# A two-block transformer in float32: the last phase worked by token tile, weights split in place, the expert loop's end rearranged

## What is computed

```python
x = x + hier_moe(rms_norm(x, ffn_norm), ...)          # experts
x = rms_norm(x, final_norm)
for i in range(2):
    h = x @ w_in[i]                                   # 7 or 10 chunks of 256 columns
    mix = gmlp_mixer(u, v, ...) if i == 0 else moba_attention(q, k, v)
    mem_out = memory_cross_attention(q_mem, mem, w_mem_kv[i])
    sub = concatenate([mix, mem_out]) @ w_mix_out[i]
    x = layer_norm(ALPHA * x + sub, ln_mix_g[i], ln_mix_b[i])
    g, u = split(x @ w_ffn_in[i])
    x = layer_norm(ALPHA * x + (silu(g) * u) @ w_ffn_out[i], ln_ffn_g[i], ln_ffn_b[i])
```

## Time and profile before

| | us |
|---|---|
| median of 3 runs | 1829.1 |
| runs, lowest to highest | 1827.12 to 1831.46 |
| the profiled execution's own time | 1827.96 |
| its span (first to last instruction) | 1826.5 |
| PE busy (matmuls) in the span | 1409.8, 77% |
| DVE, ACT, POOL busy | 605.9, 412.3, 58.6 |

### The profile page before, as it was taken

How to read it: one execution, slowest core, us unless ns; L and a number is a source line. 1 busy time by engine, 2 the same in 40 slices (tenths; PEclk the granted TensorE clock), 3 DMA queues, 4 the chain that set the end, 5 groups by cost and what they waited for, 6 DMA issues and landing times. The chain is left out here.

```text
span 1826.5 us, 21480 instructions
## 1 busy us (share of the span) xinstructions
PE 1409.8 (77%) x9510; PEld 988.7 (54%) x9510; DVE 605.9 (33%) x777; ACT 412.3 (23%) x551; POOL 58.6 (3%) x78
## 2 busy tenths in 40 slices
PE   7998876787565666566566656678899989979997
PEld 7987733343122212222222212368799979879996
DVE  5566611001010110011001100256744465674445
ACT  4544300000000000000000000154344334434332
POOL 3000000000000000000000000010200020020001
PEclk9998988987888878887878787879899989999999
DMA  9432779999999999999999999773655534345540
GB/s 305 143 139 80 321 319 422 423 420 413 421 421 422 421 421 421 421 421 422 421 421 421 421 422 421 316 241 104 204 192 177 196 104 160 116 151 195 185 162 24
DMA packets 153452, 540.13 MB, mean 296 GB/s; under 512 B 8496, under 2 KB 90768, under 8 KB 103952
## 3 DMA queue, kind: packets, MB, share of 16 engines
q1 hardware_dynamic: 152768, 537.18, 75.4%
q10 hardware_dynamic: 592, 1.58, 0.2%
HBM read 537.69 MB, written 1.05 MB: 295 GB/s over the span
## 5 line engine op out<-in xcount | busy, mean ns | idle before, releaser
L1611 PE MATMUL bank<-big,xe 128*32 128x512 f32 x2032 | 322.2, 789 | 244.7 <-DMA big<-in_w_dram 244.1
L1611 PEld LDWEIGHTS bank<-big,xe 128*32 128x32 f32 x2032 | 86.6, 139 | 477.1 <-issue 476.2
L260 DVE TENSOR_TENSOR lo<-raw,hi 128x2048 fp32r<-128x2048 f32 (+1 forms) x114 | 260.5, 2291 | 220.7 <-ACT hi L253 220.7
L101 PE MATMUL bank<-xT,hi 128*128 128x256 f32 x880 | 255.4, 290 | 18.0 <-DVE xT L1133 17.5
L102 PE MATMUL bank<-xT,hi 128*128 128x256 f32 x880 | 253.2, 288 | 0.0
L103 PE MATMUL bank<-xT,lo 128*128 128x256 f32 x880 | 253.1, 288 | 0.0
L253 ACT CAST hi<-raw 128x2048 fp32r<-128x2048 f32 (+1 forms) x114 | 216.2, 1902 | 54.1 <-PE bank L103 48.9
L1717 DVE TENSOR_TENSOR x<-bank,x 128x512 f32<-128x512 f32 x64 | 44.3, 692 | 525.5 <-PE bank L1575 525.5
L101 PEld LDWEIGHTS bank<-xT,hi 128*128 128x128 f32 x880 | 173.2, 197 | 21.8 <-issue 10.6
L102 PEld LDWEIGHTS bank<-xT,hi 128*128 128x128 f32 x880 | 173.2, 197 | 0.7
L103 PEld LDWEIGHTS bank<-xT,lo 128*128 128x128 f32 x880 | 173.2, 197 | 0.0
(11 more groups left out here) (333 smaller groups left out, 1726.5 us busy)
## 6 DMA issues: line engine op xcount, KB each, us to landing
big<-in_w_dram SPq DMA_DIRECT2D x191, 2048.0 KB, 25.9
raw<-in_w_ffn_in_dram SPq DMA_DIRECT2D x44, 1024.0 KB, 5.2
raw<-in_w_ffn_out_dram SPq DMA_DIRECT2D x22, 1024.0 KB, 5.0
raw<-in_w_in_dram SPq DMA_DIRECT2D x16, 1024.0 KB, 9.4
raw<-in_b_w_in_dram SPq DMA_DIRECT2D x10, 1024.0 KB, 5.2
raw<-in_w_mix_out_dram SPq DMA_DIRECT2D x8, 1024.0 KB, 8.9
raw<-in_a_w_in_dram SPq DMA_DIRECT2D x7, 1024.0 KB, 13.2
raw<-in_w_out_dram SPq DMA_DIRECT2D x4, 1024.0 KB, 4.9
```

The costliest lines, as they stand in the source:

```text
L101: self.matmul(out, ah, bl, start=start, stop=False)
L260: dve.tensor_tensor(self.lo_[i % NB][:, 0:k], self.raw_[self.slot(i)][:, 0:k], self.hi_[i % NB][:, 0:k].bitcast(F32), ALU.subtract).then_i ...
L1611: last = pe.matmul(hb.t[32 * e:32 * e + 32, :], xe[:, k, 32 * e:32 * e + 32], each[e][:, r * 512:(r + 1) * 512], start=(k == 0), stop=(k = ...
```

## The change

- **Norms by token tile.** In the last phase every norm is done for tile 0, then for tile 1. The last three `onto` chunks of a product (two in the second mixer) are first all done for tile 0, then all for tile 1 (`tail`); the transposes of tile 0 stand after the first chunk's part for tile 1. The next product begins with four chunks (`lead`): each for tile 0, with the transposes of tile 1 between the second and third, and then each for tile 1. A chunk whose weights are stationary (`across_tile`) so takes 96 matmuls with 128 moving columns in place of 48 with 256; one whose activations are stationary (`down_tile`) keeps its 48 of 256. The leads hold 1, 4, 3 and 4 `across` chunks (norms 0 to 3), the first and third lead also 3 and 1 `down` chunks. ACT now evicts the transposes with gain and bias (eight activations of 128 columns a tile) and makes the hi half, DVE makes the lo half.
- **Weights split in place.** `Stream` has 8 `raw` slots, lo is written over raw, and 4 `hi` slots; a load waits for the slot's last use by PE in place of its split.
- **POOL is out of the last phase.** DVE computes the residual x (`onward`) inside the feed-forward and the attention; of the last norm it does both tiles.
- **First mixer.** v's three chunks are in the lead, its norm (`normed_v`) precedes the memory attention, u's three chunks fill the attention. Of the second mixer the first four input chunks are in the lead, the other six are in steps 1, 3, ... 11 of the attention.
- **End of the round.** The gather for q = 16 is gone from a round, as are the barrier and clearing; they stand in `between_rounds`, which a branch on all engines at the loop's head skips in the first round. The last group's y, combine and norm are in the last phase; y's copies wait for one half each. The first two chunks of the last phase are loaded into memory of their own before the experts' first load, the others as soon as the experts' last users let their slots go.

Core of the diff:

```diff
+        def across_tile(b, wh, wl, n, t):
+            at = slice(t * P, (t + 1) * P)
+            for c in range(KT):
+                pe.wait_ge(*s["xT"].of((n, t, c // 4)))
+                for j in range(2):
+                    k = slice(j * P, (j + 1) * P)
+                    last = pe.mm3(b[:, j * S + t * P:j * S + (t + 1) * P], wh[:, c, k], wl[:, c, k], xh[:, c, at],
+                                  xl[:, c, at], c + j == 0, c + j == KT)
+            return last
+        def lead(n, four):
+            got = []
+            for k, (part, name, evicted) in enumerate(four):
+                if k == 2:
+                    turn(n, 1)
+                wh, wl, i = w.get(pe)
+                b = ps.take(name, evicted, name, hold=True)
+                pe.wait_ge(*b.was)
+                part(b.t, wh, wl, n, 0)
+                got.append((part, name, b.t, wh, wl, i))
+            for part, name, b, wh, wl, i in got:
+                part(b, wh, wl, n, 1).then_inc(*s["used_b"].up(i, name))
+                ps.let(name)
+        def tail(n, banks, name, parts):
+            got = []
+            for k, (src, c0, ready) in enumerate(parts):
+                wh, wl, i = w.get(pe)
+                end = k == len(parts) - 1
+                last = onto_tile((wh, wl), banks, src, name, c0, 0, False, end, ready)
...
+            for k, (src, c0, ready) in enumerate(parts):
+                wl_, i = got[k]
+                end = k == len(parts) - 1
+                onto_tile(wl_, banks, src, name, c0, 1, False, end, ready).then_inc(
+                    *s["used_b"].up(i, *([(name, 3)] if end else [])))
+                if k == 0 and n < 4:
+                    turn(n, 0)
         def ffn(layer):
...
+            n, name, banks = 2 * layer + 1, ("ffn", layer), {}
+            lead(n, [(across_tile, (k, layer, i), s[e]) for i in range(2) for k, e in (("g", "silu"), ("u", "f"))])
...
+            onto(banks, *part(0)[0:1], name, 0, True, part(0)[2])
+            for i in range(2, self.n_f):
+                whole(across_tile, ("g", layer, i), s["silu"], n)
+                whole(across_tile, ("u", layer, i), s["f"], n)
+                if i < self.n_f - 2:
+                    onto(banks, *part(i - 1)[0:1], name, 0, False, part(i - 1)[2])
+            tail(n + 1, banks, name, [part(i) for i in range(self.n_f - 3, self.n_f)])
...
+        def norm(n, name, k):
+            split()
+            normed(n, 0, name)
+            lower_x(n, 0)
+            for _ in range(k - 1):
+                split()
+            normed(n, 1, name)
+            lower_x(n, 1)
...
-                with nc.sync.If(rnd > 0):
-                    self.reload_round()
-                in_round()
+                with nc.If(rnd > 0):
+                    now, self.ps = self.ps, s.round_end
+                    self.between_rounds()
+                    self.ps = now
+                one_round()
```

More of the change, by code:

```diff
@@ L197, in let, with copy @@
     def let(self, key):
-        self.held[self.where[key]] = False
+        self.free.append(self.where[key])
+    def copy(self):
+        other = Psum(self.tensors)
+        other.where = dict(self.where)
+        return other
     def of(self, key):
@@ L389, in memory_map @@
[L389 to L394, removed]
+    m.qmT = region("qmT", 2 * S)
+    assert m.top <= free_m
+    m.wb = [region(f"wb{i}", 512, 12 * half if i == 0 else None) for i in range(2)]
@@ L696, in sp_first @@
             self.w_a.load(sp, i)
+        for i in range(2):
+            self.w_b.load(sp, i)
         def free(i):
@@ L1647, in pe_round @@
                                              start=(c + r == 0), stop=(c + r == 2))
[L1648 to L1661, removed]
+                    last.then_inc(*(used.up(("y", q, 0, c)) if h == 0 else used.up(*chunk, ("y", q, 1, c), ("down", q))))
     def act_round(self):
-        act, ps, m, s, w = self.act, self.ps, self.m, self.s, self.w_b
+        act, ps, m, s = self.act, self.ps, self.m, self.s
         act.wait_ge(*s["rounds"].of("all"))
@@ L1738, in dve_round @@
                                           *s["m_ws"].up(i))
[L1740 to L1756, removed]
@@ new lines, in onto_tile @@
+        def onto_tile(wl_, banks, src, name, c0, t, begin, end, ready):
+            wh, wl = wl_
+            sh, sl = src
+            order = [(c, h) for h in range(2) for c in range(2)] if end else [(c, h) for c in range(2) for h in range(2)]
+            at = slice(t * P, (t + 1) * P)
+            for c, h in order:
+                k = 2 * t + h
+                if k not in banks:
+                    b = ps.take((name, k), s["z"], (name, k), hold=True)
+                    pe.wait_ge(*b.was)
+                    banks[k] = b.t[:, :]
+                for signal, point in ready(c0 + c, t):
+                    pe.wait_ge(*signal.of(point))
+                half = slice(h * 512, (h + 1) * 512)
+                last = pe.mm3(banks[k], sh[:, c0 + c, at], sl[:, c0 + c, at], wh[:, c, half], wl[:, c, half],
+                              begin and c == 0, end and c == 1)
+                if end and c == 1:
+                    ps.let((name, k))
+                    if h == 0:
+                        last.then_inc(*s["used_b"].up((name, k)))
+            return last
```

785 lines of the change are left out of this document (435 added, 350 removed).

## The result

The changed kernel takes **1909.5 us** (median of 4 runs, 1909.2 to 1911.9), the kernel before beside it 1828.1 (4 runs): ratio 1.0445, 95% interval 1.0427 to 1.0463. It is 81 us slower. The prediction said slower, but 1840, with 1862 as the upper end of its range: it holds the direction and misses 70 of the 81 us. The profiled execution has a span of 1907.9 us against 1826.5.

The account below looks back on a forecast made before the run. The last phase was taken as bound by PE's work plus what each norm costs. Terms -14 + 5 + 10.4 + 5.6 + 10.4 - 2 - 3.8 = +11.6 on 1828.0 gave 1839.6, said as 1840 us; range 1803 to 1862.

Parts of the forecast that it names:

- The price of 128 columns: Twelve tile-split lead chunks: 96 matmuls at 0.11 us replace 48 at 0.12, +4.8 us a chunk, +58 us in all.
- fast and slow rivals: Pace of 128-column float32r matmuls: 0.067 us gives 1805, chance 0.22; 0.22 us gives 1962, chance 0.13.
- A norm in the change: Norms 1 to 3: 4.2 us of waits and transposes plus extra matmuls, against 13 each before: +10.4, +5.6, +10.4.
- PE at full clock: Expected sign at the norms: stretches without a dip, PE at full clock, a four-chunk lead of about 42 us.
- third rival: Same matmul price, but no late fourth chunk, attention saving 4, no slow clock after waits: 1828, chance 0.12.
- First mixer, +5: One `across` lead chunk +4.8, eight transposes +0.9, moved attention and v-norm waits set equal within 4: +5 us.
- the experts' end: Between experts and last phase: splits, table and barrier leave the path, first product at 1189: -14 us.
- Second mixer and rest of norm 2: Attention's last units needed only by tile 1, 5 us later: -2 (+3 to -4); norm 2: +5.6.
- The end, -3.8: After PE's last matmul only tile 1 is left: 7.3 us to the end instead of 11.1, -3.8.
- The moved loads and POOL's work, 0: Last phase: loads waiting for PE's use and POOL's work moved to half-idle DVE cost nothing.
- The chance of 0.53: Chance given to the forecast's own case, 1832 to 1858 us, with a pace of 0.105 to 0.12.
- only one way to be much slower: 128-column float32r matmuls at float32's price, 0.22 us each: +127 us, 1962, chance 0.13, left outside the range.

Follow-up runs that it names:

- mid4: Kernel before, chunks i = 4 and 5 of each feed-forward (8 in all) computed as two runs of 128 columns: 1871.2 us, ratio 1.0218.
- att0: Changed kernel with all lead chunks taken whole, and output-weight splits placed later in the first mixer's attention: 1828.7 us, ratio 0.9991.
- split2: Changed kernel with only the first two chunks of each lead taken by tile, the others whole: 1868.0 us, ratio 1.0198.
- mid4w12: mid4 plus a PE wait ahead of chunk i = 4 of each feed-forward, made by 12 repeats of a DVE operation: 1924.3 us, ratio 1.0503.
- before4: Kernel before, the first four chunks of each feed-forward (8 in all) computed as two runs of 128 columns: 1944.1 us, ratio 1.0616.
- midw12: Kernel before plus the same wait as mid4w12, all chunks kept 256 columns wide: 1845.2 us, ratio 1.0072.
- split3: Changed kernel with the first three chunks of each lead taken by tile and the fourth whole: 1834.8 us, ratio 1.0027.

## Why the prediction was wrong, step by step

- **The price of 128 columns: right.** 0.11 us a start at full clock, 5.0 us a chunk in mid4 against 4.8. The Trainium skill's TensorE: Matmul & The Clock Gate gives 81 ns in "Back-to-back issue gap", and its "LDWEIGHTS" makes 107 of 128 columns; the trace decides for the second. Both fast and slow rivals (0.067 and 0.22 us) fall, although 0.21 does appear, for another reason.
- **"A norm in the change": the step that failed.** It forecast the wait of 2 us in front of the fourth chunk (measured 2.69), priced it at 2 us, and took every product of the lead at full clock. A lead was to take 4 x 10.6 + 0.9 + 2 = 45.3 us; it took 71.0 both times (1291.6 to 1362.6, 1664.3 to 1735.3), 25.7 more, of which 0.7 is the wait's own size. With the 3.1 and 2.5 us at half clock behind the leads this makes **54 of the 70 us missed**. The prediction had slow stretches before it, in the 13 us of the norms of the kernel before (6.8 to 10.2 us long), but no term of its own norms has one, and it looked for "PE at full clock" there. How long such a stretch lasts is set by what stands behind the wait. The prediction's third rival counts "the slow clock after each wait" only as something to be won back. The first wait, for tile 0's scaling, was forecast at 0.4 us and took 1.91, 0.52 and 2.25.
- **First mixer, +5: mis-sized.** The first product came at 1189.7, forecast 1189, so **the experts' end** gave its 14 us. They were lost again before norm 1: taking out the 2.1 us wait for tile 0 and its transposes (0.9), the output products end at 1288.7, where 1278.3 was forecast. That is +10 us, and the two traces give 9.5 of it. From the first product to the last of these output products PE is idle for 11.3 us (tile 0's wait left out), against 5.5 before, mainly by the 9.57 us in the attention. Its products run at half clock for 16.4 us against 9.0, which costs 3.7 more. The waits were "set equal, within 4" without looking at what VectorE queues between the steps. att0 shows 3.2 us to be the order of the splits; the rest was not tried.
- **Second mixer and rest of norm 2:** from lead to lead 134.7 us, by the forecast's terms 132.5; half clock for 3.4 us at 1550 and again at 1659 is of that size.
- **The end, -3.8: right.** 7.4 us from the end of PE's last product to the end, forecast 7.3.
- **The moved loads and POOL's work, 0: right as far as it shows.** In the full-clock stretch of the first feed-forward PE is busy for 116.30 of 116.30 us, and DMA's share there is 0.59, 0.58 before.

Sum of the misses, from lead to lead: the first lead begins at 1291.6, forecast 1279.6 (10 for the first mixer, the rest for the wait of 1.91); from lead 1 to lead 2 it is 238.0 us, forecast 210.2; from there to lead 3 134.7, forecast 132.5; from lead 3 to the end 243.6, forecast 215.8. That is 12.0 + 27.8 + 2.2 + 27.8 = 69.8 us, and 51.4 of it (2 x 25.7) lie inside the two leads.

The chance of 0.53 was on a case with the right mechanism of each single product and without the one that ties them together. The upper end, 1862, left no room for it, since the prediction knew only one way to be much slower.

## What to carry to other kernels

Cutting work finer to fill a wait has two prices: more instructions, if each costs the same below some size, and a place where a small wait can stand in front of a long run of the small ones. Here the second (54 us) was as large as the first (58 us). Put wide products (256 columns or more here) directly behind a wait of PE, and keep a short run of narrow ones out of its shadow. When PE is busy all the time and still slow, look at the granted clock of the stretch before looking for work. And a cover that costs as much as what it covers (three tiled chunks against one bare norm) is no gain even when it works perfectly.

## What the runs showed of the hardware

- Half clock outlasts the wait that began it by as long as 128-column float32r products follow: 20.5 to 23.9 us for 96 of them (split2), 44 to 48 for 192 (mid4w12), 88.7 for 384 (before4), against 3 to 17 us, the wait's own part included, where 256- or 512-column products follow in these runs from norm 1 on. The Trainium skill's TensorE: Matmul & The Clock Gate, "Why this matters for your kernels", asks for TensorE to be kept busy and for no idle gaps between bursts. The gaps of 5.41 us agree with it, each was followed by a fall; those of 2.69 us are shorter than the ones that it warns of, and were followed by a fall as well. That busy alone brings full clock does not agree: before4 has PE busy for 87.27 of 88.70 us at 0.50. Busy is here what the profile's records cover, latency included, and does not tell how many columns pass.
- Not every wait brings the clock down. Those of 5.41 us all did (mid4w12 and midw12, two each); of those of 1.9 to 2.7 us some did and some did not (1.91, 2.25, 2.27 and 2.68 us above). What decides it is not shown.
- The narrow products don't bring the clock down themselves: 288 of them with no gap of PE among them in split3, and four chunks of them in each feed-forward of mid4, kept full clock.
- At half clock a 128-column and a 256-column product start at the same distance, 0.21 us (mid4w12 and midw12, behind the wait), at full clock 0.11 and 0.12: at either level it hardly matters for these weights whether there are 128 columns or 256.
- Why the width of the products decides when the clock comes back is not shown by these runs, nor where between 128 and 256 columns it turns.
